# Loads reordered at the start, state stores moved up, and the last combine with the sample first and four output buffers

## The chip, the cores and the metric

One Trainium2 chip; the program runs on one of its cores. The metric is the device time of one execution in microseconds (us). The engines are TensorE (PE; its weight loads are shown as PEld), VectorE (DVE), ScalarE (ACT), GpSimd (POOL) and SyncE (SP), which issues nearly all DMAs here. A core has 16 DMA engines.

## What is computed

One inference step of a decoder layer, for 1024 prompt tokens and 8 sample tokens (one for each of 8 sequences) that share all weights; the width D is 1024, everything is float32.

```python
mod = silu(c) @ w_ada + b_ada                         # 9 rows of c: 1 prompt, 8 samples; w_ada 1024 x 6144
sh1, sc1, g1, sh2, sc2, g2 = split(mod, 6)
h = rms_norm(x, norm1_g) * (1 + sc1) + sh1
z = h @ w_in                                          # 1024 x 3080: q k v o, 2 x 4 gates, glu a and b
hm, C, n, m = mlstm_chunkwise(q, k, v, gates, state)  # 4 heads of 128, chunks of 128 tokens; C and n are outputs
hc = swish(layer_norm(causal_depthwise_conv31(a * sigmoid(b))))
x = x + g1 * (concat(norm(hm) * sigmoid(o), hc) @ w_out)
h2 = rms_norm(x, norm2_g) * (1 + sc2) + sh2
x = x + g2 * HierMoE(h2)                              # best of 4 groups, then 2 of its 8 experts; 32 experts of width 256
y = rms_norm(x, final_g)
```

## The kernel before

Tokens are cut into nine row tiles: tiles 0 to 7 hold 128 prompt tokens each, tile 8 (`NC_`) the 8 sample tokens. Every engine has its own program, and the order on each is written out by hand; engines meet only at semaphores. All products that matter are made from a high part and a low remainder of each operand (`whi`/`wlo`, `hhi`/`hlo`, `ehi`/`elo`): ScalarE writes the high part, VectorE subtracts it for the low part, and TensorE makes three products (high by high, high by low, low by high).

**Start (the ramp).** SP issues in this order: `c` (2 loads), ten small vectors, and then, tile by tile, a row tile `xt` (512 KB, two buffers; from the third on SP waits for `xn_done`, the tile normalised two before) and a group of `w_ada` (`ada_load`, 1024 KB, eight buffers `wada`). Behind the last pair come the two halves of the first `w_in` block (`wraw`, 1024 KB each), `wgt` (the gate columns of `w_in`, 32 bytes a piece) and `m0t`. For each tile ScalarE makes the root mean square (L1778 to L1780), VectorE scales the tile (`xnorm`, L1885), TensorE turns it (L2036) and VectorE copies it into `hf` (L1900); TensorE then adds the tile's group of `w_ada` into the modulations (`ada(0, t)`, L2020). After the eighth group ScalarE first splits the first `w_in` block (`hi(0)`, L1798, which needs `wraw`), then copies the modulations out of PSUM, four copies of 9 rows (`mod_rows`, L1790). TensorE turns them (L2027), VectorE adds the bias and makes the factor `A1` (L1907, L1916), and block after block of `hf` is scaled, split into `hhi` (ScalarE, L1823) and `hlo` (VectorE, `h_lo`, L1933).

**Projections.** `project(j)`, j = 0 to 23, waits for `whi` and `wlo` of its block and makes 8 x 3 x 3 matmuls (L2053). VectorE computes the convolution beside it. The second and third group of eight `w_ada` loads are issued while projections 0 to 3 and 4 to 7 run, and used behind them.

**First stage's end.** Eight chunks of the recurrence run with the output projection (L931) and the router; VectorE makes x (`tile_x2`) and h2 (`tile_h2`), SP stores both in DRAM (`store_tile`), tiles in the order 0 to 6, 8, 7. There is one h2 buffer. After the last store SP stores the state C (256 KB) and n (2 KB, the column `caug[:, :, DH]`, so one element at a time), both from `caug`, and then issues the experts' first weights (`moe_loads`). VectorE waits for all these stores and the logits (L1349), sets `stage1_over`, and waits for GpSimd's index row `ioti` (L1180), which it casts into `iot` (L1353). On `stage1_over` GpSimd also clears `xg` (L1181). The routing follows, all on VectorE, and after it the experts.

**Experts.** 36 rounds (32 experts and overflow): GpSimd gathers rows of h2 (L1192), TensorE makes gate and up (L1561) and down (L1580), GpSimd scatters the results to DRAM (L1212). Weights have four buffers.

**Last combine.** For each tile SP loads the pair of expert results `y12` (1024 KB, four buffers) and the rows of x (`x2_load`); TensorE sums the pair by two diagonal matrices (L1628), VectorE multiplies by the gate and adds x (L1530, L1533), ScalarE squares into the output buffer and makes the root (L1323 to L1325), VectorE scales (`scaled`, L1516), SP stores (`y_out`). The order is `last`: tile 0, the sample, tiles 1 to 7. `of` has two buffers, so the square of the third tile waits for the store of the first.

## Time and profile before

| what | us |
|---|---|
| median of 3 runs (1101.33 to 1107.74) | 1107.31 |
| profiled execution, its own time | 1115.27 |
| its span, from the first to the last instruction | 1113.5 |
| TensorE busy | 975.8 (88%) |
| VectorE busy | 753.9 (68%) |
| ScalarE busy | 510.1 (46%) |
| GpSimd busy | 240.1 (22%) |

An engine is busy while an instruction of its own runs; matmuls are pipelined and their ends are modelled. The mean granted clock of TensorE is 0.922 of its full rate. A row of a timeline gives the start, the time, engine, line and operation, output<-input, the number of instructions merged into the row, and in brackets how long the engine had been idle and what released it.

### The profile page before, as it was taken

How to read it: one execution, taken by the hardware profiler on the slowest of the kernel's cores; microseconds unless marked ns; L12 is line 12 of the kernel's file. 1: busy time of each engine (PE TensorE's matmuls, PEld its weight loads, DVE VectorE, ACT ScalarE, POOL GpSimd, SP SyncE). 2: the span in 40 equal slices, each digit the busy share in tenths (PEclk: the TensorE clock that was granted, in tenths of full speed). 3: DMA queues.
4: the chain of work that ended last, by engine and by line, in shares of the span. 5: the costliest groups of instructions: out<-in, count | busy, mean ns of one | idle time of the engine just before them, and what ended most of it. 6: DMA issues, size and time to landing. Idle time of an engine off the chain costs nothing. (4 is left out here: it accounts for less than half of the span.)

```text
span 1113.5 us, 13179 instructions
## 1 busy us (share of the span) xinstructions
PE 975.8 (88%) x5077; PEld 786.4 (71%) x5077; DVE 753.9 (68%) x1020; ACT 510.1 (46%) x706; POOL 240.1 (22%) x261
## 2 busy tenths in 40 slices
PE   4499999999999799999998724899999899999764
PEld 2298979899999667665554424688888778888521
DVE  3450129988999925445542349699999689999547
ACT  4451241132121633432322103588888688888524
POOL 0000000000000000000000003366667756666320
PEclk9699999999999986989989856899999989999877
DMA  7953711112110720111114193599999979997585
GB/s 275 379 204 114 281 39 38 39 3 73 39 38 1 245 62 19 60 57 58 57 57 136 66 270 151 215 374 390 363 404 372 376 298 385 399 367 281 204 337 208
DMA packets 65491, 215.37 MB, mean 193 GB/s; under 512 B 14304, under 2 KB 35440, under 8 KB 47230
## 3 DMA queue, kind: packets, MB, share of 16 engines
q1 hardware_dynamic: 54622, 197.52, 47.9%
q0 software_dynamic: 10800, 16.93, 4.2%
q8 instruction: 43, 0.70, 0.3%
q14 instruction: 26, 0.21, 0.1%
HBM read 202.81 MB, written 34.49 MB: 213 GB/s over the span
## 5 line engine op out<-in xcount | busy, mean ns | idle before, releaser
L1344 DVE TENSOR_TENSOR elo<-eraw,ehi 128x1024 fp32r<-128x1024 f32 x148 | 174.2, 1220 | 0.0
L1962 DVE SCALAR_TENSOR_TENSOR z<-z,wdT 128x1024 f32<-128x1024 f32 x120 | 144.7, 1279 | 0.0
L1253 ACT ACTIVATE ehi<-eraw 128x1024 fp32r<-128x1024 f32 x148 | 144.6, 1068 | 0.0
L2053 PE MATMUL ps<-hhi,whi 128*128 128x344 f32 x576 | 124.2, 324 | 6.2 <-ACT hhi L1823 3.2
L2053 PE MATMUL ps<-hhi,wlo 128*128 128x344 f32 x576 | 123.5, 323 | 0.0
L2053 PE MATMUL ps<-hlo,whi 128*128 128x344 f32 x576 | 122.8, 322 | 0.0
L1804 ACT ACTIVATE z<-ps 128x1032 f32<-128x1032 f32 x24 | 24.8, 1035 | 212.7 <-PE ps L2053 203.5
L2053 PEld LDWEIGHTS ps<-hhi,whi 128*128 128x128 f32 x576 | 98.1, 191 | 9.0 <-issue 6.0
L1180 POOL IOTA ioti<- 128x128 int32 x1 | 0.2, 240 | 482.8 <-DVE marks L1330 482.8
L2053 PEld LDWEIGHTS ps<-hhi,wlo 128*128 128x128 f32 x576 | 98.6, 191 | 0.0
L2053 PEld LDWEIGHTS ps<-hlo,whi 128*128 128x128 f32 x576 | 97.0, 190 | 0.2 <-DVE hlo L1933 0.2
L1480 DVE TENSOR_TENSOR dlo<-draw,dhi 128x2048 fp32r<-128x2048 f32 x36 | 82.6, 2295 | 12.0 <-ACT dhi L1259 11.9
L1891 DVE TENSOR_TENSOR wlo<-wraw,whi 128x1024 fp32r<-128x1024 f32 x24 | 29.4, 1223 | 86.0 <-ACT whi L1798 86.0
L1561 PE MATMUL ps<-ehi,xhi 128*128 128x512 f32 x288 | 77.5, 413 | 0.0
L1561 PE MATMUL ps<-ehi,xlo 128*128 128x512 f32 x288 | 71.2, 389 | 0.0
L1561 PE MATMUL ps<-elo,xhi 128*128 128x512 f32 x288 | 71.1, 389 | 0.0
L1259 ACT ACTIVATE dhi<-draw 128x2048 fp32r<-128x2048 f32 x36 | 68.8, 1912 | 3.7 <-DMA draw<-in_w_down 3.7
L1212 POOL DMA_INDIRECT expert_results<-ysb,scur x36 | 61.5, 1707 | 7.3 <-issue 7.3
L1561 PEld LDWEIGHTS ps<-ehi,xlo 128*128 128x128 f32 x288 | 54.2, 188 | 11.4
L1561 PEld LDWEIGHTS ps<-elo,xhi 128*128 128x128 f32 x288 | 54.1, 188 | 11.2
L931 PE MATMUL ps<-wout,featT 128*128 128x512 f32 x128 | 59.5, 620 | 2.7 <-ACT bcv L441 2.7
L1465 DVE TENSOR_TENSOR xlo<-ps,xhi 128x1024 fp32r<-128x1024 f32 x37 | 45.3, 1224 | 22.5 <-ACT xhi L1263 22.5
(393 smaller groups left out, 1699.6 us busy)
## 6 DMA issues: line engine op xcount, KB each, us to landing
eraw<-in_w_gate SPq DMA_DIRECT2D x37, 1024.0 KB, 7.7
eraw<-in_w_up SPq DMA_DIRECT2D x37, 1024.0 KB, 13.1
draw<-in_w_down SPq DMA_DIRECT2D x36, 1024.0 KB, 12.8
wada<-in_w_ada SPq DMA_DIRECT2D x24, 1024.0 KB, 9.6
wraw<-in_w_in SPq DMA_DIRECT2D x12, 1024.0 KB, 5.4
y<-expert_results SPq DMA_DIRECT2D x8, 1024.0 KB, 8.2
xt<-in_x_prompt SPq DMA_DIRECT2D x8, 512.0 KB, 5.8
wout<-in_w_out SPq DMA_DIRECT2D x1, 4096.0 KB, 15.6
```

The costliest lines, as they stand in the source:

```text
L931: mm = pe.matmul(ps[:, YB + a, :], lhs, wout[:, k, a * 512:(a + 1) * 512], start=(k == 0), stop=(k == KD - 1))
L1212: pool.indirect_dma_start(out=ye_dram, in_=ysb[:, b, :], in_offset=None, out_offset=bass.IndirectOffsetOnAxis(ap=scur[:, b, :], axis=0), b ...
L1253: act.activation(ehi[:, b, :, k, :], eraw[:, wb(e), :, k, :], ACT.Copy).then_inc(sem("ehi_ready"), 1)
L1259: act.activation(dhi[:, b, :, :], draw[:, db(e), :, :], ACT.Copy).then_inc(sem("dhi_ready"), 1)
L1344: dve.tensor_tensor(elo[:, wb(e), :, k, :], eraw[:, wb(e), :, k, :], ehi[:, b, :, k, :].bitcast(F32), ALU.subtract)\
L1465: dve.tensor_tensor(xlo[:, b, :, :], ps[:, 0:2, :].rearrange("p a (k n) -> p (a k) n", k=4), xhi[:, b, :, :].bitcast(F32), ALU.subtract).t ...
L1480: dve.tensor_tensor(dlo[:, db(e), :, :], draw[:, db(e), :, :], dhi[:, b, :, :].bitcast(F32), ALU.subtract)\
L1561: mm = pe.matmul(ps[:, 2, :], x[:, b, k, :], w[:, at, :, k, :], start=(i + k == 0), stop=(i == 2 and k == KD - 1))
L1804: act.activation(z[:, j, PAD:ZW].rearrange("p (c n) -> p c n", c=3), ps[:, 3 * v:3 * v + 3, 0:TW], ACT.Sigmoid if j >= O0 else ACT.Copy).t ...
L1891: dve.tensor_tensor(wlo[:, u, :, block], wraw[:, u, :, block], whi[:, j % 2, :, :].bitcast(F32), ALU.subtract)\
L1962: dve.scalar_tensor_tensor(out=z[:, GB0 + b, PAD:SC], in0=z[:, U0 + b, w:w + T], scalar=wdT[:, b, w:w + 1], in1=z[:, GB0 + b, PAD:SC], op0 ...
L2053: mm = pe.matmul(ps[0:n, bank + c, 0:TW], w(k), h[:, k, c * TW:(c + 1) * TW], start=first, stop=last)
```

## The change

The ten small vectors are issued behind row tile 3, the row tiles have four buffers, and `wraw` is issued only when groups 6 and 7 of `w_ada` have landed; `wgt` and `m0t` go behind the fourth half of `w_in`. TensorE uses group t - 1 of `w_ada` behind tile t, and turns the small vectors at tile 5. The first modulations are copied out by ScalarE (two rows of four) before it splits `w_in`, and by VectorE (the other two); `w_lo(0)` goes behind the first scaled block. C and n are stored behind the last row load of the first stage. The index row is made at the program's start and cast behind `mlstm_done`. In the combine the sample goes first, its loads too, and the output has four buffers. Buffers are placed anew for that.

```diff
@@ -111,7 +111,7 @@
     order = list(range(NC_ - 1)) + [NC_, NC_ - 1]
-    last = [0, NC_] + list(range(1, NC_))
+    last = [NC_] + list(range(NC_))
     x2_dram = nc.dram_tensor("x2_scratch", (NTOK, D), F32, kind="Internal").ap()
@@ -197,10 +199,10 @@
         wdw = sb(stA, "wdw", [CW, CB * P])
-        xt = sb(stA, "xt", [P, 2, D])
+        xt = sb(stA, "xt", [P, 4, D])
         xn = sb(stA, "xn", [P, 2, D])
...
-        taken = D + P + CB * P + 4 * D
+        taken = D + P + CB * P + 6 * D
         sb(stA, "blocks_0_7", [P, 8 * ZW - taken])
@@ -312,8 +312,10 @@
         y12 = sb(st3, "y12", [P, FB, 2, D])
-        of = sb(st3, "of", [P, 2, D])
         xf = sb(st3, "xf", [P, 5, D])
...
+        sb(st3, "rows_and_down_weights", [P, 11, D])
+        of = sb(st3, "of", [P, 4, D])
         ys = ysb[0:S, :, :]
@@ -775,6 +777,8 @@
             dve.memset(mark(), 0.0).then_inc(step("mlstm_done"), 1)
+            dve.wait_ge(step("iota_ready"), after("iota_ready"))
+            chain.last(dve.tensor_copy(iot[:, :], ioti[:, :]))
             for j in range(NC_ - 2, NT):
@@ -1155,29 +1159,28 @@
                 sp.wait_ge(sem("of_ready"), j + 1)
-                sp.dma_start(y_d[t], of[0:rows[t], j % 2, :]).then_inc(sem(f"y_out{j % 2}"), 16)
...
-            y12_load(0)
+                sp.dma_start(y_d[t], of[0:rows[t], j % 4, :]).then_inc(sem(f"y_out{j % 4}"), 16)
...
             x2_load(NC_)
-            for t in range(1, FB):
+            for t in range(FB):
                 y12_load(t)
...
                         x2_load(t)
-                if j + FB < NC_:
-                    y12_load(j + FB)
+                if 1 <= j <= NC_ - FB:
+                    y12_load(j + FB - 1)
                 if j:
...
             for s, v in (("out_done", 16 * 4), ("m_out", 32), ("c_out", 64), ("state_out", 32), ("x2_out1", 16 * 4),
-                         ("h2_out", 16 * NT), ("y_out0", 16 * 5), ("y_out1", 16 * 4)):
+                         ("h2_out", 16 * NT), ("y_out0", 16 * 3), ("y_out1", 16 * 2), ("y_out2", 16 * 2),
+                         ("y_out3", 16 * 2)):
                 sp.wait_ge(sem(s), v)
...
             pool.wait_ge(step("stage1_over"), after("stage1_over"))
-            pool.iota(ioti[:, :], pattern=[[1, P]], base=0, channel_multiplier=0).then_inc(step("iota_ready"), 1)
             pool.memset(xg[:, :, :], 0.0).then_inc(sem("xg_zero"), 1)
@@ -1318,9 +1321,11 @@
                 act.wait_ge(sem("xsum_ready"), j + 1)
+                if j >= 4:
+                    act.wait_ge(sem(f"y_out{j % 4}"), 16 * (j // 4))
                 if j >= 2:
-                    act.wait_ge(sem(f"y_out{b}"), 16 * (j // 2))
-                chain(act.activation(of[0:m, b, :], xrow(t)[0:m, :], ACT.Square, accum_out=ssq[0:m, b, 0:1]))
+                    act.wait_ge(sem("of_ready"), j - 1)
+                chain(act.activation(of[0:m, j % 4, :], xrow(t)[0:m, :], ACT.Square, accum_out=ssq[0:m, b, 0:1]))
                 chain(act.activation(ssq[0:m, b, 1:2], ssq[0:m, b, 0:1], ACT.Ln, bias=epst[0:m, :], scale=1.0 / D))
@@ -1349,8 +1354,7 @@
             signal("stage1_over")
-            dve.wait_ge(step("iota_ready"), after("iota_ready"))
-            chain(dve.tensor_copy(iot[:, :], ioti[:, :]))
+            dve.wait_ge(sem("logit_ready"), NT)
             experts = iot[:, 0:NE]
@@ -1639,14 +1643,16 @@
             load(c9[1:9, :], c_sample, "c_in")
-            for at, n, v in ((0, MB, b_ada), (MB, KD, norm1_g), (MB + KD, KD, norm2_g), (MB + 2 * KD, H, mh_g),
-                             (MB + 2 * KD + 4, CB, b_dw), (MB + 2 * KD + 8, CB, cln_g),
-                             (MB + 2 * KD + 12, CB, cln_b)):
-                load(vecs[at:at + n, :], v if len(v.shape) == 2 else v.rearrange("(b p) -> b p", p=P), "vec_in")
-            load(wdw[:, :], w_dw, "vec_in")
-            load(bi[:, :], b_ig.rearrange("(h o) -> h o", o=1), "gbias_in")
-            load(bf[:, :], b_fg.rearrange("(h o) -> h o", o=1), "gbias_in")
...
+            def vector_loads():
...
+                for at, n, v in ((0, MB, b_ada), (MB, KD, norm1_g), (MB + KD, KD, norm2_g), (MB + 2 * KD, H, mh_g),
+                                 (MB + 2 * KD + 4, CB, b_dw), (MB + 2 * KD + 8, CB, cln_g),
+                                 (MB + 2 * KD + 12, CB, cln_b)):
+                    load(vecs[at:at + n, :], v if len(v.shape) == 2 else v.rearrange("(b p) -> b p", p=P), "vec_in")
+                load(wdw[:, :], w_dw, "vec_in")
+                load(bi[:, :], b_ig.rearrange("(h o) -> h o", o=1), "gbias_in")
+                load(bf[:, :], b_fg.rearrange("(h o) -> h o", o=1), "gbias_in")
@@ -1655,15 +1661,16 @@
             for t in range(NT):
-                if t >= 2:
-                    sp.wait_ge(sem("xn_done"), t - 1)
-                load(xt[0:rows[t], t % 2, :], x_d[t], f"x_in{t % 2}")
+                if t >= 4:
+                    sp.wait_ge(sem("xn_done"), t - 3)
+                load(xt[0:rows[t], t % 4, :], x_d[t], f"x_in{t % 4}")
                 if t:
                     ada_load(t - 1)
-            load(wraw[:, 0, :, :], w_in_v[:, :, C0_CONV:C0_CONV + 256], "wraw_in0")
-            load(wraw[:, 1, :, :], w_in_v[:, :, C0_CONV + 256:C0_CONV + 512], "wraw_in1")
-            load(wgt[:, :, :], w_in_v[:, :, 4 * H * DH:4 * H * DH + 2 * H], "wgt_in")
-            load(m0t[:, :], m0.rearrange("b h -> h b"), "m0_in")
+                if t == 3:
+                    vector_loads()
+            for u in range(2):
+                sp.wait_ge(sem(f"wada_in{6 + u}"), 16)
+                load(wraw[:, u, :, :], w_in_v[:, :, C0_CONV + 256 * u:C0_CONV + 256 * (u + 1)], f"wraw_in{u}")
@@ -1675,6 +1682,8 @@
                 w_in_load(1, u)
+            load(wgt[:, :, :], w_in_v[:, :, 4 * H * DH:4 * H * DH + 2 * H], "wgt_in")
+            load(m0t[:, :], m0.rearrange("b h -> h b"), "m0_in")
             for n in range(2 * KD, 3 * KD):
@@ -1715,6 +1724,10 @@
                 load(x2[0:rows[t], b, :], x_d[t], f"xr_in{b}")
+                if j == NT - 1:
+                    sp.wait_ge(step("mlstm_done"), after("mlstm_done"))
+                    load(C_p.rearrange("h d e -> d h e"), caug[:, :, 0:DH], "state_out")
+                    load(n_p.rearrange("h d -> d h"), caug[:, :, DH], "state_out")
                 if j >= 1:
@@ -1725,9 +1738,6 @@
             store_tile(sp, NT - 1)
-            sp.wait_ge(step("mlstm_done"), after("mlstm_done"))
-            load(C_p.rearrange("h d e -> d h e"), caug[:, :, 0:DH], "state_out")
-            load(n_p.rearrange("h d -> d h"), caug[:, :, DH], "state_out")
             moe_loads(sp)
@@ -1748,7 +1758,7 @@
+            pool.iota(ioti[:, :], pattern=[[1, P]], base=0, channel_multiplier=0).then_inc(step("iota_ready"), 1)
@@ -1772,10 +1782,10 @@
                 b, n = t % 2, rows[t]
-                act.wait_ge(sem(f"x_in{b}"), 16 * (t // 2 + 1))
+                act.wait_ge(sem(f"x_in{t % 4}"), 16 * (t // 4 + 1))
                 if t >= 2:
                     act.wait_ge(sem("xT_done"), t - 1)
-                chain(act.activation(xn[0:n, b, :], xt[0:n, b, :], ACT.Square, accum_out=ssq[0:n, b, 0:1]))
+                chain(act.activation(xn[0:n, b, :], xt[0:n, t % 4, :], ACT.Square, accum_out=ssq[0:n, b, 0:1]))
                 chain(act.activation(ssq[0:n, b, 1:2], ssq[0:n, b, 0:1], ACT.Ln, bias=epst[0:n, :], scale=1.0 / D))
@@ -1786,7 +1796,7 @@
                     act.wait_ge(sem("modT_ps"), g)
-                for j in range(4):
+                for j in range(4 if g else 2):
                     act.activation(modr[32 * j:32 * j + 9, :], ps[32 * j:32 * j + 9, ACC[g], :], ACT.Copy)\
@@ -1812,8 +1822,8 @@
                 act.activation(mark(), epst[0:1, 0:1], ACT.Copy).then_inc(sem("z_evac"), 1)
+            mod_rows(0)
             hi(0)
-            mod_rows(0)
@@ -1875,14 +1885,11 @@
                .then_inc(step("c9T_ready"), 1)
-            dve.wait_ge(step("vT_ps"), after("vT_ps"))
-            chain.last(dve.tensor_copy(vT[:, :], ps[:, 5, 0:NV]))
-            chain(dve.tensor_copy(wdT[:, :, :], ps[:, 5, P:P + 32 * CB].rearrange("p (b w) -> p b w", b=CB)[:, :, 0:CW]))
...
                 dve.wait_ge(sem("rstd_ready"), t + 1)
-                dve.tensor_scalar(xn[0:n, b, :], xt[0:n, b, :], ssq[0:n, b, 1:2], None, ALU.mult)\
+                dve.tensor_scalar(xn[0:n, b, :], xt[0:n, t % 4, :], ssq[0:n, b, 1:2], None, ALU.mult)\
                    .then_inc(sem("xn_done"), 1)
@@ -1900,6 +1907,11 @@
                    .then_inc(sem("xT_copied"), 1)
+                if t == 5:
+                    dve.wait_ge(step("vT_ps"), after("vT_ps"))
+                    chain.last(dve.tensor_copy(vT[:, :], ps[:, 5, 0:NV]))
+                    chain.last(dve.tensor_copy(wdT[:, :, :],
+                                               ps[:, 5, P:P + 32 * CB].rearrange("p (b w) -> p b w", b=CB)[:, :, 0:CW]))
@@ -1919,7 +1931,10 @@
             chain.wait()
-            w_lo(0)
+            dve.wait_ge(sem("ada_used"), KD)
+            dve.wait_ge(step("modr_zero"), after("modr_zero"))
+            for j in range(2, 4):
+                dve.tensor_copy(modr[32 * j:32 * j + 9, :], ps[32 * j:32 * j + 9, ACC[0], :]).then_inc(sem("modr_ready"), 1)
             modulation(0)
@@ -1939,6 +1954,8 @@
                     h_lo(k - 1)
+                else:
+                    w_lo(0)
             h_lo(KD - 1)
@@ -2004,11 +2021,6 @@
             mm.then_inc(step("c9T_ps"), 1)
-            pe.wait_ge(sem("vec_in"), 16 * 8)
-            pe.transpose(ps[:, 5, 0:NV], vecs[:, :], ident[0:NV, 0:NV])
-            for b in range(CB):
-                mm = pe.transpose(ps[:, 5, P + 32 * b:P + 32 * b + CW], wdw[:, b * P:(b + 1) * P], ident[0:CW, 0:CW])
-            mm.then_inc(step("vT_ps"), 1)
             pe.wait_ge(step("c9T_ready"), after("c9T_ready"))
@@ -2036,8 +2048,15 @@
                 mm.then_inc(sem("xT_done"), 1)
-                if t < KD:
-                    ada(0, t)
+                if t:
+                    ada(0, t - 1)
+                if t == 5:
+                    pe.wait_ge(sem("vec_in"), 16 * 8)
+                    pe.transpose(ps[:, 5, 0:NV], vecs[:, :], ident[0:NV, 0:NV])
+                    for b in range(CB):
+                        mm = pe.transpose(ps[:, 5, P + 32 * b:P + 32 * b + CW], wdw[:, b * P:(b + 1) * P],
+                                          ident[0:CW, 0:CW])
+                    mm.then_inc(step("vT_ps"), 1)
             ada_transpose(0)
```

## Rows read from the trace of the kernel before

**Rows 1.** Stretches: us, busy us by engine (instructions), granted clock, DMA share, GB/s.
```profile
5.00:15.00 10.00, 2.96 (x16) 2.42 (x15) 2.17 (x5) 3.68 (x9) 0.00 (x0) 1.00 0.64 229
15.00:40.00 25.00, 16.34 (x101) 7.55 (x104) 12.06 (x13) 10.84 (x25) 0.00 (x0) 0.86 1.01 400
40.00:45.00 5.00, 3.16 (x30) 1.34 (x23) 2.54 (x3) 0.88 (x6) 0.00 (x0) 1.00 1.04 358
```

**Rows 2.** Timeline of TensorE's first projection.
```profile
54.41 1.20 PE L2053 MATMUL ps<-hhi,whi 128*128 128x344 f32 x3 [3.22 <-ACT hhi L1823]
...
57.12 1.06 PE L2053 MATMUL ps<-hhi,whi 128*128 128x344 f32 x3
...
62.23 0.62 PE L2053 MATMUL ps<-hhi,whi 128*128 128x344 f32 x3
```

**Rows 3.** Timeline of the start, all engines (SPq: SP issuing a DMA).
```profile
1.22 0.29 SPq L1638 DMA_DIRECT2D c<-in_c_sample  x1
...
3.14 1.05 ACT L1769 ACTIVATE c<-c 9x1024 f32<-9x1024 f32 x1 [1.06 <-DMA c<-in_c_sample]
...
38.33 5.25 SPq L1638 DMA_DIRECT2D wgt<-in_w_in  x1
...
43.66 1.04 PE L2020 MATMUL ps<-wada,c9T 128*9 128x512 f32 x8 [1.84 <-DMA wada<-in_w_ada]
...
47.61 2.41 ACT L1790 ACTIVATE modr<-ps 9x512 f32<-9x512 f32 x4
...
52.35 0.81 DVE L1939 TENSOR_SCALAR hf<-hf,A,modT 128x1024 f32<-128x1024 f32 x1
```

**Rows 4.** The page's costliest groups: count, busy us, mean ns, idle us before.
```profile
L2053 PE MATMUL ps<-hhi,whi 128*128 128x344 f32 x576 | 124.2, 324 | 6.2 <-ACT hhi L1823 3.2
```

**Rows 5.** Timeline of the first stage's end and the routing.
```profile
609.79 0.97 PEld L948 LDWEIGHTS ps<-ident,h 128*128 128x128 f32 x8 [0.91 <-DVE h L700]
...
636.67 0.34 SPq L329 DMA_DIRECT2D h_scratch<-h  x1
...
643.45 0.20 DVE L705 TENSOR_TENSOR logits<-ps,rbias 128x36 f32<-128x36 f32 x1 [6.71 <-PE ps L962]
...
650.16 0.06 DVE L1330 MEMSET marks<- 1x1 f32 x1 [6.52 <-DMA out<-caug]
...
650.48 1.81 POOL L1181 MEMSET xg<- 128x2048 f32 x1
650.57 1.80 DVE L1353 CAST iot<-ioti 128x128 f32<-128x128 int32 x1 [0.35 <-POOL ioti L1180]
...
676.72 0.28 DVE L1437 TENSOR_SCALAR ohp<-iot,lent 128x128 f32<-128x128 f32 x1
```

**Rows 6.** DMA issues: count, KB each, median us from issue to landing.
```profile
x_scratch<-x SPq DMA_DIRECT2D x8, 512.0 KB, 2.6
...
out<-caug SPq DMA_DIRECT2D x1, 2.0 KB, 12.6
```

**Rows 7.** Timeline of the last combine.
```profile
1066.94 30.57 PE L1628 MATMUL ps<-y,dg 128*128 128x512 f32 x64 [11.19 <-DMA y<-expert_results]
...
1073.62 1.23 DVE L1530 TENSOR_TENSOR ps<-ps,g2b 128x1024 f32<-128x1024 f32 x1 [12.56 <-PE ps L1628]
...
1100.91 1.23 DVE L1530 TENSOR_TENSOR ps<-ps,g2b 128x1024 f32<-128x1024 f32 x1
...
1104.50 1.23 DVE L1530 TENSOR_TENSOR ps<-ps,g2b 128x1024 f32<-128x1024 f32 x1
```

**Rows 8.** The chain that ended last: start us, us, what.
```profile
874.21 11.76 DMA expert_results<-ysb,scur
...
1081.14 5.96 DMA out<-of
```

**Rows 9.** Timeline of VectorE at the end of the first projection.
```profile
66.19 1.23 DVE L1933 TENSOR_TENSOR hlo<-hf,hhi 128x1032 fp32r<-128x1032 f32 x1 [0.80 <-ACT hhi L1823]
```

8 lines of the change are left out of this document (4 added, 4 removed).

## The prediction

> **What bounds the kernel now.** I read the stretches of the start first, then the order of time there, then the same for the two other places that the edits touch: the hand-over from the first stage to the experts, and the last 50 us. In all three nothing that the change touches runs at its engine's pace; a transfer, or a wait that a transfer ends, sets the end.
>
> *Start.* From 15 to 40 us the 16 DMA engines are full (share 1.01, 400 GB/s); between 5 and 15 us they are not (0.64, 229 GB/s) [rows 1]. SP waits there for a free row buffer before it may issue. TensorE's first projection starts at 54.41 [rows 2], 10.75 us after the last w_ada product starts (43.66, and that had waited for its DMA) [rows 3]. In between ScalarE waits for the first w_in half, splits it, and only then copies the four rows of modulations out of PSUM from 47.61 on, 2.41 us for four [rows 3]. In the projections TensorE hardly waits (6.2 us idle before the 576 products of the first kind, all at their start [rows 4]), so whatever their start gains, their end gains.
>
> *Hand-over.* The last logits are there at 643.45 + 0.20, but VectorE passes on only at 650.16, released by the store out<-caug (issued behind the last h2 store, which goes at 636.67), then casts the index row for 1.80 us, beside a GpSimd memset of 1.81 us [rows 5]. The n store is 2 KB, one element at a time, and takes 12.6 us to land [rows 6]. The routing behind it is one chain on VectorE that everything waits for.
>
> *Last stretch.* TensorE combines from 1066.94 for 30.57 us, so its last tile is done at 1097.5; VectorE begins its last tile only at 1104.50, 3.59 us after the one before [rows 7]. The chain of waits passes at 1081.14 through the store out<-of for 5.96 us [rows 8]: ScalarE has two output buffers, and the third square waits for the first store to land.
>
> **The change, part by part.** The sum is made against the profiled execution (1115.27 us, span 1113.5), which lies 8 us above the median shown; I take the gain off the median 1107.31.
>
> *Ramp: when the last w_ada group lands.* Nine row tiles and eight w_ada groups are 12,320 KB = 12.6 MB, with the small vectors 12.7 MB. Four row buffers instead of two put x0 to x3 and three groups (5.2 MB) in the queue before SP waits at all, and each later pair is released by a tile normalised three tiles earlier, so I count on a queue that never runs dry. A small load takes 1.9 us from issue to use (1.22 to 3.14 [rows 3]); the rows now follow it directly, so bytes flow from 3.2. At 400 GB/s, 12.7 MB take 31.8 us: 35.0. The first w_in half is released when group 6 has landed and shares the engines with group 7: 0 to 2.6 us, I take half, 1.3. Group 7 then lands at 36.3, 7.35 us earlier than 43.66. Bounds: at 358 GB/s, the row of 40 to 45 [rows 1], it lands at 40.0 (3.65 earlier); without sharing at 35.0 (8.65). I take 400 because that stretch has the same transfers in it.
>
> *Ramp: from there to the first projection.* The 2.91 us between the last product's end (43.66 + 1.04) and the first PSUM copy go, since ScalarE now copies before it splits. Two copies on ScalarE beside two on VectorE, at 0.60 each on both, take 1.2 for 2.41: another 1.2. w_lo(0) comes back in: it now starts behind the first hf multiply (ending at 52.35 + 0.81 = 53.16 [rows 3]) and takes 1.23, as the subtraction in [rows 9] does, so it ends about where TensorE starts now (54.41): nothing at the start. Behind it VectorE's eight hlo subtractions are late by 1.2; their cover is ScalarE, for which VectorE already waits 0.80 before the last one [rows 9]; should ScalarE gain pace, up to 1.2 would show. Splitting w_in needs its half landed (36.3 + 2.6 = 38.9 by the sum above) before ScalarE's first hhi: 3.14 us lie between the last PSUM copy's end (47.61 + 2.41) and hf's first block, so that is due at 36.3 + 1.04 + 1.2 + 3.14 = 41.7, and the split hides beside the modulation arithmetic. Gain of this part 4.1, less 0.4 for the cover not being whole: 3.7. **Ramp 11.0** (7.4 to 12.7).
>
> *What moves in the queue at the start.* The ten small vectors go behind 5.2 MB, 13 us, and are first needed at tile 5; their transposes and copies go into gaps that TensorE spends waiting for w_ada. wgt and m0 (5.25 us of SP's time for the first [rows 3]) move behind the fourth w_in half; queued behind them is the third w_ada group: 6 us plus 8.4 MB at 400 GB/s is 27 us, against four whole projections of TensorE, at 24 groups of 0.62 [rows 2] less overlap. Nothing. w_ada's second group is issued later by SP's two new waits, but not needed before four projections either.
>
> *Hand-over.* The C and n stores go behind the last row load, which follows the store of the h that is ready at 609.79 [rows 5]; issued by 611, at 12.6 us they land by 624, and SP's next work is the sample tile's store. They cost nothing while that holds. VectorE then waits for the logits, 643.65, and for the last h2 store, issued at 636.7. Its landing is in no row; an x2 store of that size takes 2.6 [rows 6], so 639.3, and the 12.6 of the n store would bound it at 649.3. The cast left the chain; the memset did not. Routing starts behind the cast at 652.37 now; after the change, if the memset (0.15 behind the mark, 1.81 long) holds VectorE as it held the cast, at 645.65: 6.7 earlier; if not, at 643.7: 8.65. I take 6.7, as the cast's 1.80 beside the memset is the only row with both. The cast itself moves to 603 us, with GpSimd idle, and there it is on the path, for TensorE waits for VectorE's h at 609.79 [rows 5]. Its price: 0.28, as a 128x128 operation takes at 676.72, without GpSimd, up to the cast's 1.80 [rows 5]. I take 0.28, the row without GpSimd. **Hand-over 6.4** (-0.7 to 8.4, the low end with h2's store and the cast at their bounds).
> The Trainium skill (SBUF — State Buffer, "SBUF: two separate sides") says that VectorE in a two-port mode and GpSimd exclude each other on one port pair for a whole instruction, and that an operation with two SBUF inputs is held only by a GpSimd operation that reads. The cast's row agrees; by that rule a reduce and a compare of the routing would pass the memset and this part would give 6.9 instead of 6.4.
>
> *Last stretch.* The sample's load goes ahead of the first pair, so TensorE starts about 0.6 later (two issues like the 0.29 at 1.22 [rows 3]): first result 1074.2 for 1073.62. The sample's first three VectorE operations fall into the wait before that; seven further tiles of 3.59 put the last tile at 1099.4 instead of 1104.50. Four output buffers take the wait for the store away; next late is VectorE itself, with TensorE's last tile (1098.1) 1.3 us ahead. Low end: rows of tiles 6 and 7 now load ahead of pair 4, 1 MB or 2.6 us; high end TensorE's pace, 6.4. **Last stretch 5.1** (2.5 to 6.4).
>
> Sum 11.0 + 6.4 + 5.1 = 22.5: 1092.8 for the profiled execution, **1084.8** by the median. In the experts' stage nothing changes but its start.
>
> **Rivals.**
> A, *the full queue is slower than I take*: group 7 lands at 40.0 and the ramp gives 7.4; sum 18.9, 1088.4. For it the row of 358 GB/s; against it 400 over 25 us. The Trainium skill (DMA: Bandwidth & Descriptors, "Where 436 GB/s comes from") says that the HBM side, about 358 GB/s for a core, binds loads; the 25 us at 400 on this one core speak against it. 0.13.
> B, *the last h2 store takes the state stores' place*: 6 MB of expert weights are issued right behind it. If it lands 6 us late the hand-over gives nothing: sum 16.1, 1091.2. Against it: it is ahead of them in the queue. 0.08.
> C, *given back*: the ramp keeps only its 3.7, because rows and groups in a deep queue delay each other, and the experts' stage dips once more. It has one dip now, at 874.21, where the chain of waits passes through a scatter of 11.76 us [rows 8]; a second would take up to that. Sum 3.7 + 6.4 + 5.1 - 11.8 = 3.4, 1103.9: no change. Against: both orders start the experts with every weight buffer full. 0.09.
> D, *slower, by the clock of TensorE*: three products take 1.06 at the lower level (1.2 GHz) at 57.12 and 0.62 at the higher (2.4 GHz) at 62.23 [rows 2]. A projection of 24 such groups costs up to 10.6 more at the lower level. If the shorter, denser ramp left TensorE at 1.2 GHz for longer, from two projections on the whole gain would be gone, and from the fourth it is over 1% slower: 42.4 lost, 22.5 gained, 1127. For it: the granted clock was 0.86 over 15 to 40 us [rows 1]. Against: after the pause before 54.41 the higher level was back by 62.23, within the first projection. 0.03.
>
> **How the numbers follow.** The forecast has 0.67. All terms at their good ends give 27.5 (1079.8), at their poor ends 9.2; poor ends of all three at once I leave out, and take about 14 (1093). The runs shown spread by 6.4, so I widen by 2 to 3 on each side: 1076 to 1096, which takes in A and B. What a measurement of this kernel can tell from no change is about 1%, 11.1 us. Faster by more: forecast, A and B, 0.88; within: C, 0.09; slower: D, 0.03.
>
> **What would show it.** Last w_ada product at 36 to 37 and the first projection at 43 to 44, with DMA share at 1.0 from 5 us on; row loads four ahead. out<-caug issued about 25 us before the last h2 store, VectorE's routing 6 to 9 us closer to the last logits, the cast near 0.3. In the last stretch no ScalarE wait for an output store, and 3.6 us per tile from the first result to the last. Wrong would be: w_ada products that still wait for their DMA until 40, routing that waits for h2's store, or a combine in which TensorE waits for pair 4.

## The result and the profile after

The changed kernel takes 1090.11 us (median of 4 runs, 1085.23 to 1092.95) against 1107.53 for the kernel before, measured beside it: a ratio of 0.984, 95% interval 0.981 to 0.987, so 17.4 us or 1.6% faster. The prediction had 1084.8 within 1076 to 1096, and 0.88 on faster by over 1%. The profiled execution took 1090.31 us (span 1088.6, mean granted clock 0.932), 25.0 less than the one shown of before (1115.27). Two of all executions, one of the kernel before (2479 us) and one of stores_late (3369 us), were disturbed, and the ratios and the table below leave them out; the 4.5 for stores_late in a later expectation has it in.

*Start.* Stretches of the changed kernel; they answer to [rows 1]:
```profile
5.00:15.00 10.00, 7.07 (x43) 4.54 (x42) 4.85 (x6) 6.46 (x15) 0.00 (x0) 1.00 1.03 428
15.00:33.00 18.00, 11.40 (x69) 5.80 (x69) 7.88 (x10) 6.30 (x15) 0.00 (x0) 0.81 1.02 407
33.00:40.00 7.00, 3.70 (x32) 1.66 (x32) 4.38 (x6) 3.17 (x11) 0.00 (x0) 1.00 0.70 222
```
The queue is full from 5 us on, at the rate that I had taken, and thins out from 33 us. The timeline of the same start, against [rows 2, 3]:
```profile
35.01 2.96 SPq L1642 DMA_DIRECT2D wraw<-in_w_in  x2
35.20 1.06 ACT L1788 ACTIVATE xn<-xt 8x1024 f32<-8x1024 f32 x1 [1.36 <-DMA xt<-in_x_sample]
...
37.74 0.66 PE L2048 MATMUL ps<-ident,xn 8*128 8x8 f32 x8 [0.99 <-DVE xn L1892]
...
38.33 1.05 PE L2032 MATMUL ps<-wada,c9T 128*9 128x512 f32 x8
39.45 1.20 ACT L1800 ACTIVATE modr<-ps 9x512 f32<-9x512 f32 x2 [2.35 <-PE ps L2032]
39.51 1.42 DVE L1937 COPY modr<-ps 9x512 f32<-9x512 f32 x2 [0.56 <-issue]
40.67 1.06 ACT L1808 ACTIVATE whi<-wraw 128x1024 fp32r<-128x1024 f32 x1
...
43.53 1.22 DVE L1898 TENSOR_TENSOR wlo<-wraw,whi 128x1024 fp32r<-128x1024 f32 x1
...
44.86 1.20 PE L2072 MATMUL ps<-hhi,whi 128*128 128x344 f32 x3 [3.22 <-DVE wlo L1898]
```
The last w_ada product starts at 38.33 instead of 43.66, and it no longer waits for its load: it stands behind the sample tile's transposes (37.74). The first projection starts at 44.86 instead of 54.41. TensorE's idle time before the 576 products is 6.2 us as in [rows 4]. The projections end at 356.08 instead of 364.27, so of the 9.6 us at their start 8.2 are left at their end; they take 309.9 to 311.4 us in all the traces, with either start.

*Hand-over.* Timeline of the changed kernel, against [rows 5]:
```profile
591.40 0.22 DVE L781 CAST iot<-ioti 128x128 f32<-128x128 int32 x1
...
599.21 1.44 SPq L1642 DMA_DIRECT2D out<-caug  x2
...
626.91 0.35 SPq L331 DMA_DIRECT2D h_scratch<-h  x1
...
633.69 0.20 DVE L707 TENSOR_TENSOR logits<-ps,rbias 128x36 f32<-128x36 f32 x1 [6.71 <-PE ps L966]
633.98 0.06 DVE L1335 MEMSET marks<- 1x1 f32 x1
633.99 0.19 DVE L1363 TENSOR_REDUCE r<-logits 128x9 f32<-128x36 f32 x1
634.10 1.81 POOL L1184 MEMSET xg<- 128x2048 f32 x1 [475.55 <-DVE marks L1335]
634.22 0.20 DVE L1364 TENSOR_TENSOR gb_<-logits,r 128x36 f32<-128x36 f32 x1
634.45 1.50 DVE L1366 TENSOR_SCALAR gb_<-gb_ 128x36 f32<-128x36 f32 x1
```
The mark (633.98) follows the last logits at once; before it came 6.5 us behind them. The cast takes 0.22 instead of 1.80. But the first tensor_scalar of the routing takes 1.50 and ends with GpSimd's memset (634.10 + 1.81 = 635.91), while the reduce and the compare ahead of it, which read logits, take 0.19 and 0.20.

*Last stretch.* Timeline of the combine, against [rows 7]; the experts' end is at 1042.21 here and was at 1061.01:
```profile
1048.52 30.54 PE L1632 MATMUL ps<-y,dg 128*128 128x512 f32 x64 [11.60 <-DMA y<-expert_results]
...
1054.56 1.23 DVE L1534 TENSOR_TENSOR ps<-ps,g2b 128x1024 f32<-128x1024 f32 x1 [4.46 <-PE ps L1632]
...
1076.12 1.22 DVE L1534 TENSOR_TENSOR ps<-ps,g2b 128x1024 f32<-128x1024 f32 x1
...
1079.71 1.22 DVE L1534 TENSOR_TENSOR ps<-ps,g2b 128x1024 f32<-128x1024 f32 x1
...
1083.96 1.28 DVE L1520 SCALAR_TENSOR_TENSOR of<-xf,ssq,fgb 128x1024 f32<-128x1024 f32 x1 [0.58 <-ACT ssq L1330]
```
From the first result to the last tile VectorE goes 3.59 us a tile (25.15 / 7), without a stop. In the chain that ended last the experts' stage still has one dip, as in [rows 8], and no store of an output:
```profile
857.58 11.34 DMA expert_results<-ysb,scur
```

### The profile page after: what moved, and what is told of

It reads as the page before. It is cut to its first block, busy times and chain, and to the rows that moved or that the text cites. A ratio compares the mean times of both kernels' runs of the same rounds, so it can differ in the third digit from the quotient of the medians.

```text
span 1088.6 us, 13179 instructions
## 1 busy us (share of the span) xinstructions
PE 972.5 (89%) x5077; PEld 784.7 (72%) x5077; DVE 754.0 (69%) x1022; ACT 509.1 (47%) x704; POOL 240.2 (22%) x261
## 4 chain that ended last, share of the span: by engine, by line
PE 46%; DVE 8%; issue 4%; DMA 3%; POOL 2%; ACT 2%; SPq 0%; POOLq 0%; DVEq 0%; ACTq 0%
PE ps L1565 15%; PE ps L935 10%; PE ps L1584 7%; PE ps L1552 3%; DMA expert_results<-ysb,scur 1%; DVE elo L1349 1%; PE ps L875 1%; POOL dg L1205 1%; DMA draw<-in_w_down 1%; PE ps L1030 1%; DVE ps L1534 1%; PE ps L1035 1%; PE ps L952 1%; DVE ps L687 1%; PE ps L1600 1%
## 6 DMA issues: line engine op xcount, KB each, us to landing
eraw<-in_w_up SPq DMA_DIRECT2D x37, 1024.0 KB, 12.8
wada<-in_w_ada SPq DMA_DIRECT2D x24, 1024.0 KB, 13.9
```

## The experiments

Single executions of the kernel before lie up to 14 us apart (1101.33 to 1115.27), so each place was read in the traces too. In the table, *first* is the start of the first projection, *stage* the time from there to the last logits, *wait* from the start of the last logits to the routing's first reduce, and *last* from the experts' end to the start of the last scaled tile, each the difference of two timeline rows; the ratio is to the kernel before, with its 95% interval.

| kernel | median us | ratio | first | stage | wait | last |
|---|---|---|---|---|---|---|
| before (trace shown) | 1107.5 | 1 | 54.41 | 589.0 | 8.95 | 48.04 |
| before_again | 1109.0 | 1.002 (1.000 to 1.004) | 52.91 | 587.1 | 8.66 | 48.08 |
| changed | 1090.1 | 0.984 (0.981 to 0.987) | 44.86 | 588.8 | 0.30 | 41.75 |
| after_again | 1089.9 | 0.984 (0.980 to 0.988) | 45.23 | 587.1 | 0.30 | 41.28 |
| start_undone | 1096.8 | 0.989 (0.987 to 0.992) | 52.85 | 580.2 | 0.31 | 41.53 |
| start_only | 1102.4 | 0.996 (0.994 to 0.998) | 45.79 | 588.7 | 7.55 | 47.96 |
| modr_undone | 1091.6 | 0.985 (0.980 to 0.989) | 48.66 | 588.8 | 0.30 | 41.67 |
| stores_late | 1093.8 | 0.987 (0.984 to 0.990) | 45.50 | 585.6 | 7.16 | 41.56 |
| combine_undone | 1093.7 | 0.986 (0.983 to 0.988) | 45.31 | 587.0 | 0.31 | 48.09 |
| four_only | 1091.0 | 0.986 (0.981 to 0.991) | 44.89 | 581.3 | 0.31 | 45.36 |
| sample_only | 1089.6 | 0.985 (0.982 to 0.988) | 44.86 | 584.2 | 0.29 | 46.25 |
| better | 1088.0 | 0.981 (0.978 to 0.984) | 45.02 | 588.4 | 0.30 | 40.95 |
| no_wraw_wait | 1085.5 | 0.981 (0.977 to 0.984) | 46.25 | 590.2 | 0.31 | 41.26 |
| best | 1085.0 | 0.981 (0.978 to 0.984) | 44.41 | 581.3 | 0.31 | 41.90 |

### One part undone at a time

**start_undone**: all edits of the start taken back.
```diff
-            mod_rows(0)
             hi(0)
+            mod_rows(0)
...
-                if t >= 4:
-                    sp.wait_ge(sem("xn_done"), t - 3)
-                load(xt[0:rows[t], t % 4, :], x_d[t], f"x_in{t % 4}")
+                if t >= 2:
+                    sp.wait_ge(sem("xn_done"), t - 1)
+                load(xt[0:rows[t], t % 2, :], x_d[t], f"x_in{t % 2}")
```


> The changed kernel with the whole start as it was before (small vectors first, two row buffers in use, group t of w_ada behind tile t, w_in split ahead of the four copies of the modulations); hand-over and combine stay changed. Theory (the start is worth what the two traces show, 54.41 - 44.86 = 9.55 us, and nothing gives it back): 1090.1 + 9.6 = 1099.7 us, first projection at 54.4, and the distance from there to the last logits as in the changed kernel (633.69 - 44.86 = 588.8). Rival (the projections or the first stage's end give most of it back, since convolution and recurrence have their own pace): at most 1094, and a distance from first projection to last logits shorter by 5 or more. Rival of my sum (11.0 from the start): 1101.1.

The first projection came at 52.85, 8.0 later than in the changed kernel, and not 9.55. The median rose by 6.7, within its scatter of both 8.0 and the 5.8 that its mean gives (1095.66 against 1089.84 over the ten runs of the changed kernel). The traced execution itself took 1090.2: its *stage* was 580.2, 8.6 shorter than in the changed kernel, so a single trace's end says nothing of the part that was undone.

**stores_late**: the stores of C and n behind the last h2 store again.
```diff
-                if j == NT - 1:
-                    sp.wait_ge(step("mlstm_done"), after("mlstm_done"))
-                    load(C_p.rearrange("h d e -> d h e"), caug[:, :, 0:DH], "state_out")
...
             store_tile(sp, NT - 1)
+            sp.wait_ge(step("mlstm_done"), after("mlstm_done"))
+            load(C_p.rearrange("h d e -> d h e"), caug[:, :, 0:DH], "state_out")
```


> The changed kernel with the stores of C and n issued behind the last h2 store again, and nothing else undone (the cast stays early). Theory: the last landing of out<-caug holds VectorE again, 6.3 us behind the last logits (before: 643.85 to 650.16), and the expert loads are issued about 2 us later, which hides: 1090.1 + 6.3 = 1096.4 us. Rival (another store, the last of h2, ends the wait anyway, so the place of the state stores is free): at most 1092, and the mark behind the logits at +0.3 as now.

The wait is back: the first reduce comes 7.16 behind the last logits instead of 0.30, 6.9 us. The time rose by 3.7, where the theory had 6.3. The rival, that the last h2 store or the expert loads would take the place of the state stores, is excluded by the pair of traces: that store is issued at 626.91 in the changed kernel and holds nothing at 633.98.

**combine_undone**: order, loads and two buffers of the combine as before.
```diff
-    last = [NC_] + list(range(NC_))
+    last = [0, NC_] + list(range(1, NC_))
...
-        of = sb(st3, "of", [P, 4, D])
+        of = sb(st3, "of", [P, 2, D])
```


> The changed kernel with the last combine as before (tile 0, the sample, tiles 1 to 7; two output buffers). Theory: the third square waits for the first store again, and from the experts' end to the last scaled tile it takes 48.0 us instead of 41.75: 1090.1 + 6.3 = 1096.4 us (5.1 by my sum: 1095.2). Rival (the loads of the pairs or TensorE set the pace, and the wait for the store falls into their slack): at most 1092.

The stretch took 48.09 instead of 41.75, as the theory said; the time rose by 3.5, less than these 6.3. The three parts undone singly cost 13.9 by medians and 8.0 + 6.9 + 6.3 = 21.2 by the traces of the three places. All three medians lie below their places, and no run shows why.

### The split of the start and of the combine

**modr_undone**: the queue as changed, the copies of the modulations and the place of `w_lo(0)` as before.
```diff
-            mod_rows(0)
             hi(0)
+            mod_rows(0)
...
-                for j in range(4 if g else 2):
+                for j in range(4):
```


> The changed kernel with the copies of the first modulations as before: all four on ScalarE, behind the split of the first w_in block, and the low part of that block (w_lo(0)) ahead of the modulation arithmetic; the queue stays as changed. Theory (this half of the start is worth 3.7, as my sum has it): ScalarE waits for the first half of w_in (landing at about 40.9), splits it, and copies from 42.0; four copies of 0.6 and the rest of the way (54.41 - 47.61 = 6.8) put the first projection at 48.8 instead of 44.86: 1094.0 us. Rival (the queue alone gave it, as the split is hidden once the load is early): first projection under 46, at most 1091.5.

First projection at 48.66, 3.8 later; the theory had 48.8. The rows of this kernel show the old order's wait:
```profile
40.90 1.06 ACT L1808 ACTIVATE whi<-wraw 128x1024 fp32r<-128x1024 f32 x1 [3.67 <-DMA wraw<-in_w_in]
41.86 2.41 ACT L1800 ACTIVATE modr<-ps 9x512 f32<-9x512 f32 x4
...
48.66 1.20 PE L2067 MATMUL ps<-hhi,whi 128*128 128x344 f32 x3 [3.22 <-ACT hhi L1833]
```

**four_only** and **sample_only**: each half of the combine's change without the other.
```diff
# four_only: order and loads as before, four buffers kept
-    last = [NC_] + list(range(NC_))
+    last = [0, NC_] + list(range(1, NC_))
# sample_only: two buffers again
-                sp.dma_start(y_d[t], of[0:rows[t], j % 4, :]).then_inc(sem(f"y_out{j % 4}"), 16)
+                sp.dma_start(y_d[t], of[0:rows[t], j % 2, :]).then_inc(sem(f"y_out{j % 2}"), 16)
```


> The changed kernel with four output buffers, but the combine's order and loads as before (tile 0, the sample, tiles 1 to 7). Theory (the gain of 6.3 in the last stretch is two things: the sample's own VectorE time of 3.8 to 4.2, which falls into the wait for the first pair only when the sample goes first, and 1.84 + 0.3 that VectorE waited behind the stores): from the experts' end to the last scaled tile 45.9 us, between 48.05 (before) and 41.75 (after): 1094 us. Rival (the stores were the bound, and the order is worth nothing): 41.75 to 42.5, 1090.5. Rival (the order is all of it): 48.

> The changed kernel with the sample's order and loads first in the combine, but two output buffers as before. With four buffers and the old order the stretch took 45.36 us, between 48.05 and 41.75. Theory (the two gains add: the order 3.6, the buffers 2.1 to 2.7, by VectorE's wait behind a late square): from the experts' end to the last scaled tile 43.9, ScalarE's square of the fourth tile waits for a store. Rival (with the sample first the stores have slack, and four buffers give nothing more): 41.3 to 42.

Four buffers alone: 45.36, 2.7 less than before (expected 45.9). The order alone: 46.25, only 1.8 less, and neither theory had that (43.9 or 41.3 to 42). In sample_only the third square waits already, for the store of the sample, which VectorE scales only behind the sum of tile 0. VectorE's timeline there shows that it waits for a root three times ahead of the last tile:
```profile
1061.46 1.28 DVE L1517 SCALAR_TENSOR_TENSOR of<-draw,ssq,fgb 128x1024 f32<-128x1024 f32 x1 [2.17 <-ACT ssq L1327]
...
1066.03 1.29 DVE L1517 SCALAR_TENSOR_TENSOR of<-draw,ssq,fgb 128x1024 f32<-128x1024 f32 x1 [0.88 <-ACT ssq L1327]
...
1074.27 1.28 DVE L1517 SCALAR_TENSOR_TENSOR of<-xf,ssq,fgb 128x1024 f32<-128x1024 f32 x1 [0.84 <-ACT ssq L1327]
```
ScalarE's timeline of the same kernel shows what its third and fourth squares wait for:
```profile
1059.72 1.06 ACT L1325 ACTIVATE of<-draw 128x1024 f32<-128x1024 f32 x1 [5.86 <-DMA out<-of]
...
1064.29 1.06 ACT L1325 ACTIVATE of<-draw 128x1024 f32<-128x1024 f32 x1 [2.86 <-DMA out<-of]
```
As I read it, the sample's 3.8 us of VectorE, between tiles 0 and 1, gave the stores time in the old order; without them, square, root, scaling and store of a tile do not fit into two tiles' time. So the two halves need each other: 1.8 and 2.7 alone, 6.3 together.

### Two more moves, and the wait of w_in

**better**: GpSimd's memset behind `mask_ready`, the last w_ada group ahead of the sample tile.
```diff
-            pool.wait_ge(step("stage1_over"), after("stage1_over"))
+            pool.wait_ge(step("mask_ready"), after("mask_ready"))
             pool.memset(xg[:, :, :], 0.0).then_inc(sem("xg_zero"), 1)
...
             for t in range(NT):
                 b, n = t % 2, rows[t]
+                if t == KD:
+                    ada(0, t - 1)
                 pe.wait_ge(sem("xn_done"), t + 1)
...
-                if t:
+                if 0 < t < KD:
                     ada(0, t - 1)
```


> The changed kernel and two more moves: GpSimd clears xg behind mask_ready, where VectorE waits 2.4 us for TensorE, instead of beside the routing; and TensorE takes the last group of w_ada ahead of the sample tile's transposes instead of behind them. Theory: the routing's first tensor_scalar took 1.50 us (634.45) because GpSimd's memset held it, so it falls to 0.2 and the experts start 1.3 earlier; the last w_ada product stood behind the sample tile (37.74), not behind its load, so it starts at 36.8 instead of 38.33 and the first projection 1.1 to 1.6 earlier: 1090.1 - 2.7 = 1087.4 us. Rival for the first: the 1.50 is that instruction's own, it stays. Rival for the second: the load of group 7 lands only at about 38.3, and the product still starts there.

The rows of this kernel:
```profile
34.80 1.09 PE L2050 MATMUL ps<-ident,xn 128*128 128x128 f32 x8 [1.82 <-DVE xn L1892]
35.83 1.04 PE L2032 MATMUL ps<-wada,c9T 128*9 128x512 f32 x8
37.75 1.05 PE L2032 MATMUL ps<-wada,c9T 128*9 128x512 f32 x8 [0.87 <-DMA wada<-in_w_ada]
...
39.42 0.22 DVE L1907 COPY hf<-ps 128x64 f32<-128x64 f32 x1 [0.48 <-PE ps L2050]
39.67 1.42 DVE L1937 COPY modr<-ps 9x512 f32<-9x512 f32 x2
...
41.15 0.66 PE L2039 MATMUL ps<-ident,modr 128*128 128x128 f32 x4 [1.77 <-DVE modr L1937]
...
45.02 1.20 PE L2074 MATMUL ps<-hhi,whi 128*128 128x344 f32 x3 [3.22 <-DVE wlo L1898]
...
634.17 0.18 DVE L1366 TENSOR_SCALAR gb_<-gb_ 128x36 f32<-128x36 f32 x1
...
644.94 1.81 POOL L1184 MEMSET xg<- 128x2048 f32 x1 [486.85 <-DVE marks L1335]
```
The tensor_scalar falls from 1.50 to 0.18: it was GpSimd's memset that held it, and 1.3 us are gained there. For the second move the rival was nearer: group 7 lands only just ahead of 37.75, so the product starts 0.58 earlier, and VectorE spends that on the sample's copy, which now stands ahead of the modulations (39.42). The first projection did not come earlier.

**no_wraw_wait**: the same kernel without the waits ahead of the first w_in halves.
```diff
             for u in range(2):
-                sp.wait_ge(sem(f"wada_in{6 + u}"), 16)
                 load(wraw[:, u, :, :], w_in_v[:, :, C0_CONV + 256 * u:C0_CONV + 256 * (u + 1)], f"wraw_in{u}")
```


> The kernel of the run before called better (xg cleared behind mask_ready, last w_ada group ahead of the sample tile's transposes), and SP issues the first two halves of w_in without waiting for groups 6 and 7 of w_ada to land. Theory (the engines take the queue in its order, and group 7's late landing at 37.7 is the tail of a few lagging engines: the DMA share was 0.46 over 34 to 38 us, with room in it): group 7 still lands at 37.7 within 0.4, the first half of w_in lands over 1 us earlier, ScalarE's split loses its wait of 0.84, the first projection stays at 45.0 or comes up to 0.3 earlier; 1088.0 us. Rival (my sum's step: they share the engines, and the first half of w_in delays group 7 by 0 to 2.6, half of it 1.3): group 7 lands at 39.0, first projection 46.3, 1089.3 us.

The start's timeline in this kernel (PEld: TensorE loading weights):
```profile
24.75 9.22 SPq L1642 DMA_DIRECT2D wraw<-in_w_in  x1
...
35.01 1.91 PE L2049 MATMUL ps<-ident,xn 128*128 128x128 f32 x8 [1.93 <-DVE xn L1891]
36.84 2.71 PE L2031 MATMUL ps<-wada,c9T 128*9 128x512 f32 x16
...
38.07 0.11 PEld L2031 LDWEIGHTS ps<-wada,c9T 128*9 128x9 f32 x4 [1.10 <-DMA wada<-in_w_ada]
...
39.64 1.20 ACT L1799 ACTIVATE modr<-ps 9x512 f32<-9x512 f32 x2 [2.31 <-PE ps L2031]
...
41.91 1.12 PE L2038 MATMUL ps<-ident,modr 128*128 128x128 f32 x4 [1.76 <-DVE modr L1936]
...
46.25 1.20 PE L2073 MATMUL ps<-hhi,whi 128*128 128x344 f32 x3 [3.22 <-DVE wlo L1897]
```
TensorE's granted clock (third number from the end) from 36 to 38 us, in better and then here:
```profile
36.00:38.00 2.00, 1.13 (x12) 0.12 (x8) 0.93 (x2) 1.15 (x6) 0.00 (x0) 1.00 0.77 207
36.00:38.00 2.00, 2.00 (x13) 0.64 (x11) 0.92 (x3) 1.26 (x6) 0.00 (x0) 0.50 1.10 353
```
The first projection moves from 45.02 to 46.25, the rival's number (46.3), but not by the rival's mechanism, so the hit is luck. The weight loads for group 7 wait for its transfer until 38.07, against 37.75 for the product in better: the landing moves by 0.3, as my theory allowed, and not by 1.3. The other 0.9 is TensorE's clock, at its lower level (0.50) here where better has the higher: tile 7's transposes take 1.91 for 1.09, the products of groups 6 and 7 end at 39.55 instead of 38.80, and the four transposes of the modulations take 1.12 for 0.66. Before the fall TensorE had stood for 1.93 us (35.01), in better for 1.82 (34.80). modr_undone keeps the waits and has 0.53 over the same 2 us, so it is not shown that the waits change the clock, nor that they are worth the 1.2 us. My theory was wrong too: it had the first projection at 45.0, with no thought of the clock, and the first half of w_in over 1 us earlier, which it was not (its last part landed at 40.92, in better at 40.88). The time does not show a difference (1085.5 against 1088.0, intervals that overlap).

**best**: better, and VectorE copies its two rows of modulations ahead of the sample tile.
```diff
+                if t == NT - 1:
+                    mod_rows_dve()
                 dve.wait_ge(sem("xT_done"), t + 1)
```


> The kernel called better (xg cleared behind mask_ready, last w_ada group ahead of the sample tile's transposes; the waits of the first w_in halves stay), and VectorE copies its two rows of modulations before it copies the sample tile out of PSUM, not after. Theory: in better VectorE began these copies at 39.67, behind the sample's copy, although the last product was done at 38.80; they begin at 38.9 now, and the first projection at 44.2 to 44.4 instead of 45.02: 1087.7 - 0.7 = 1087.0 us by the mean. Rival (the first half of w_in, which landed at about 40.9, is next late: ScalarE's split ends at 42.0, VectorE's low part behind the first scaled block): 44.8 or later.

First projection at 44.41, at the edge of the 44.2 to 44.4 expected, 0.45 ahead of the changed kernel. With the memset's 1.3 that is 1.8 us by the traces of the places. The median of 1085.0 is 5 below the changed kernel's, but the intervals of the two ratios overlap, and this trace's *stage* was one of the short ones (581.3).

### The same kernels again

> The changed kernel once more, unchanged. Open is why the three parts undone singly cost 6.7 + 4.5 + 3.5 = 14.7 us by medians, while the traces give 8.0, 6.9 and 6.3 for the same three places. Theory (TensorE's granted clock in the recurrence, 395 to 500 us, wanders from one execution to the next and adds or takes some us, whatever the kernel; the three places themselves repeat): median 1090 within 2 us, first projection at 45.0 within 0.6, the mark 0.3 behind the last logits, 41.75 us within 0.3 from the experts' end to the last scaled tile, and a distance from first projection to last logits anywhere between 580 and 589. Rival (the three places themselves vary from execution to execution): one of them differs by over 1 us.

> The kernel before once more, unchanged. Its one traced execution took 1115.27 us, 8 above its median, and between its first projection and its last logits 589.0 us, against 580.2 in the trace of the changed kernel with the start undone, whose instructions there are the same. Theory (that execution was slow in the recurrence alone, where the granted clock was 0.55 over 420 to 440 us, and the three places repeat): first projection 53 to 54.5, 6.5 to 6.7 from the last logits to the mark, 48.0 within 0.4 from the experts' end to the last scaled tile, and a distance from first projection to last logits of 580 to 585 in an execution near the median. Rival (the distance is 589 in this kernel whenever it runs, and the 8 us lie in one of the three places): one of them is shorter by several us.

> The kernel before with the changed start alone (queue order, four row buffers, copies of the modulations), hand-over and combine as before. Theory A (the start's 8 to 9.5 us at the first projection stay to the end): 1108.4 - 8.5 = 1099.9 us. Theory B (part is given back: taken out of the changed kernel the start cost only 5.8 by the mean of its runs, since the recurrence runs at a lower granted clock when it starts earlier): 1102.6, and a distance from first projection to last logits some 3 us longer than in the kernel before of this call. Rival (nothing stays): 1108.

start_only is the kernel before with the edits of start_undone left in and all others taken back.

Both repeats confirm that the three places repeat: *last* within 0.5 us, *wait* within 0.3, *first* within 0.4 in the changed kernel. The 0.3 that I had set for *last* was too narrow (41.28 against 41.75), and start_only, with the old hand-over, has a *wait* of 7.55. Two larger misses count. The kernel before starts its projections at 52.91 when run again, as start_undone does (52.85):
```profile
42.17 1.05 PE L2020 MATMUL ps<-wada,c9T 128*9 128x512 f32 x8 [0.44 <-DMA wada<-in_w_ada]
...
52.91 1.20 PE L2053 MATMUL ps<-hhi,whi 128*128 128x344 f32 x3 [3.22 <-ACT hhi L1823]
```
So 1.5 us of the 54.41 in [rows 2] belonged to that execution: its last w_ada group landed at 43.6, and at 42.1 in the two others. And its *stage* of 587.1 lies above the 580 to 585 that I expected, so the recurrence of the trace shown was not as unlucky as I had said. What differs there between executions is TensorE's granted clock. The stage in start_undone and in no_wraw_wait, the shortest and the longest (last three columns: clock, DMA share, GB/s):
```profile
52.85:633.05 580.20, 549.40 (x3120) 447.68 (x3120) 346.98 (x523) 166.16 (x287) 2.25 (x5) 0.96 0.25 85
46.25:636.41 590.16, 560.36 (x3120) 457.69 (x3120) 347.16 (x522) 166.08 (x287) 2.25 (x5) 0.94 0.25 84
```
The traces also keep when the clock was at its lower level (1.2 GHz): 40.9 us of the stage in start_undone, 67.9 in no_wraw_wait. Over all 14 traces this time and the length of *stage* go together (correlation 0.99, 0.39 us of *stage* for 1 us at the lower level), and the start makes no difference to that: 58.1 us and 587.1 in before_again, 58.0 and 587.1 in after_again. The 20 us that the expectation names, in the changed kernel and then in four_only, whose edits lie behind them:
```profile
420.00:440.00 20.00, 19.88 (x70) 12.08 (x69) 12.02 (x29) 9.66 (x32) 0.00 (x0) 0.87 0.23 83
420.00:440.00 20.00, 20.00 (x87) 12.28 (x85) 11.36 (x30) 8.75 (x28) 0.00 (x0) 0.98 0.24 83
```
start_only took 1102.4: the number of its theory B (1102.6), 6.6 below before_again in the same measurement, or 4.3 by its ratio to all runs of before. But its *stage* was 588.7, 1.6 longer than in before_again and not 3, so a give-back by the clock is not shown by it.

## Why the prediction was right, and where it was off

The direction, the three places and the range were right; the forecast's sum was 22.5, the measured gain 17.4. By the traces the places add up to 21.2; that this is so near 22.5 is in part luck, for the start was put 3.0 too high and the other two 0.5 and 1.2 too low.

**Start: 11.0 forecast, 8.0 measured** (52.85 or 52.91 to 44.86). This is the term that was mis-sized.
- The base: I took 54.41 from one execution; the two others have 52.9. That is 1.5 of the 3.0.
- The landing of group 7: 36.3 in the sum, 37.7 in better, where its wait is visible, 1.4 later. The rate was right (428 and 407 GB/s against 400 taken). What failed is the step from bytes over rate to a landing. A load is there when the last of its 16 parts has landed, and the trace keeps the time of each part. Of group 7's, 15 land from 33.75 to 35.48, near the 35.0 that the bytes alone gave, and the last at 37.57; in all 11 traces with the new queue the 15th is there by 35.2 to 35.8 and the last at 37.6 to 38.1. From 35 to 36 us a sixteenth of the DMA engines' time is all that is busy (share 0.06, second number from the end):
```profile
35.00:36.00 1.00, 1.00 (x12) 0.66 (x13) 0.77 (x1) 0.80 (x1) 0.00 (x0) 1.00 0.06 25
```
  The lag comes in behind the small vectors, which now stand in the middle of the queue, a place that I had put at nothing. The group ahead of them lands within 0.5 us (15.91 to 16.41), the row tile behind them has 15 parts by 18.75 and the last at 20.95, and the loads behind that keep some 2 us of it. In the kernel before, with the vectors first, the first row tile has the same lag (15 parts by 8.50, the last at 10.51), and the third, behind SP's wait, when the queue had run empty, has none (16.12 to 16.73). No run moves the vectors alone, so that they bring the lag rests on these two orders. The 1.3 that the sum took for sharing is not shown: without the waits group 7 landed 0.3 later. I also did not see that TensorE would take the group behind the sample tile: 38.33, another 0.6.
- The path behind it: 3.7 forecast; from the product to the projection it is 10.75 us before and 6.53 now, 4.2 less, and modr_undone gives 3.8. Of the 0.5 above the forecast, 0.45 is the clock: the four transposes of the modulations take 1.11 at the lower level before (and 1.12 in modr_undone) and 0.66 at the higher one now. The cover of w_lo(0) held but for its last bit: TensorE's first projection is released by wlo, which ends at 43.53 + 1.22 = 44.75, 0.1 ahead of it.

**Hand-over: 6.4 forecast; 6.9 by stores_late,** which undoes the stores alone. With the cast behind the mark and the held tensor_scalar counted, the kernel before stands 8.95, 8.66 and 7.55 behind its logits in three executions, and the changed one 0.30 + 1.32: 5.9 to 7.3 for the whole part. The stores went out at 599.21, in the old trace's time (9.6 later) within the 611 that I had allowed, and the h2 store held nothing. The cast cost 0.22 for the 0.28 taken. On the memset I chose the wrong one of two: I let it hold VectorE from its start, and the trace shows that a reduce and a compare pass and the tensor_scalar is held. The Trainium skill (SBUF — State Buffer, "SBUF: two separate sides") says this: the port pair is taken for a whole instruction, by VectorE only in a two-port mode, or with two SBUF inputs against a GpSimd operation that reads. The trace agrees (0.19 and 0.20 beside the memset, 1.50 for the tensor_scalar, 0.18 without it). Whether 6.9 or 6.4 was the better number, 5.9 to 7.3 cannot tell.

**Last stretch: 5.1 forecast, 6.3 measured** (48.04 to 41.75). The store's wait and the sample's 3.8 us went as worked out. The first result came 12.35 behind the experts' end, where the sum had 12.61 + 0.6: 0.9. The other 0.3 is the last tile's wait for ScalarE (0.87 before, 0.58 now).

**The rest.** The places add up to 8.0 + 6.9 + 6.3 = 21.2, above the interval of the first measurement (14.7 to 20.7, from 1107.53 x 0.0133 and 0.0187) and inside that of the second (12.8 to 22.0). The *stage* between them lay at 580.2 to 589.0 with the old start (3 traces) and 581.3 to 590.2 with the new one (11 traces). The ranges cover each other, and at equal time on the lower clock level the two starts have equal stages, so it stays open whether the new start brings more of that time, some 3 us of *stage*, or whether this is chance. The experts' stage, from the routing's first reduce to the experts' end, is not the place: it took 406.8 to 409.0 us in all 14 traces.

**The rivals.** A (a queue at 358 GB/s, 1088.4) gives nearly the time, but not its mechanism: the rate was above 400 to 33 us. The Trainium skill (DMA: Bandwidth & Descriptors, "Where 436 GB/s comes from") has the HBM side, about 358 GB/s, bind such loads; the 428 and 407 GB/s of two stretches speak against it here. B is excluded by the mark at 633.98. C had a second dip in the experts' stage; there is one, 11.34 us. D had a lower clock behind the shorter ramp; the mean is 0.932 against 0.922.

## What to carry to other kernels

Base a term on the place's time in more than one execution where a transfer ends it: 1.5 us of the largest term here were one landing's own. A load's landing is not bytes over rate: it is there with the last of its 16 parts, and here a lag of some 2 us that came in behind small loads stayed in the full queue to its end. A number that comes out as a rival said does not yet show its mechanism: look at the place that the rival names. Two relaxations of one loop (an extra job taken out, buffers added) may be worth little alone and much together, so work out the loop with both.

## What the runs showed of the hardware that I had not expected

- A GpSimd memset of 1.81 us held a VectorE tensor_scalar on 36 columns for 1.50 us (0.18 when moved), and let a reduce and a tensor_tensor pass.
- With the queue full, SP spent 9.22 us on issuing one load of w_in (24.75 in no_wraw_wait), where it spent 0.37 on one behind the wait (37.71 in modr_undone).
- Behind ten small loads one of the 16 parts of each larger load landed some 2 us after the other 15, for as long as the queue stayed full (group 7: 35.48 and 37.57); where the queue had run empty the lag was gone (16.12 to 16.73 in the kernel before).
- The same stage took 580.2 us with 40.9 us of it at TensorE's lower clock level and 590.2 with 67.9; that spread is more than any one of the three parts is worth. Over 420 to 440 us the granted clock was 0.87 in the changed kernel and 0.98 in four_only, whose first projection starts 0.03 us later.
